# The low part of one weight unit moved from VectorE to GpSimd, in the last head of an mLSTM mixer

## The reference, cut to what matters

```python
ha = rmsnorm(ha, lw['norm_mlstm_h'].reshape(H_A, DV_A)).reshape(B, T, D_MODEL)
y_a = jax.nn.sigmoid(oa) * ha
...
merged = jax.nn.sigmoid(ga) * y_a + jax.nn.sigmoid(gb) * y_b
return merged @ lw['w_out'], (ckv, kr, C, n, m)
```

## Time and profile before

| | us |
|---|---|
| median of 3 runs | 1330.66 |
| lowest and highest run | 1329.96, 1330.77 |
| time of the profiled execution | 1328.88 |
| its span | 1327.2 |

### The profile page before, as it was taken

The page is one execution under the profiler, slowest core; times in us unless marked ns, Lnnn a source line. Parts: engine busy times, 40 slices in busy tenths (PEclk is TensorE's granted clock), DMA queues, the critical chain, the costliest instruction groups (busy, mean ns, idle before and its releaser), DMA issues.

```text
span 1327.2 us, 30517 instructions
## 1 busy us (share of the span) xinstructions
PE 1300.7 (98%) x11657; PEld 1232.1 (93%) x11657; DVE 959.8 (72%) x1847; ACT 602.2 (45%) x1144; POOL 145.9 (11%) x275
## 2 busy tenths in 40 slices
PE   9999999999999999999999999999999999999997
PEld 9999999999999988888888888889899999999996
DVE  5999889985487564554554665574889989988556
ACT  6455555653365344444344223324654555565323
POOL 0000000000003105555552000000000000000000
PEclk9999999999999999999999999999999999999999
DMA  4232223333156637778777323415152222333322
GB/s 177 83 126 98 96 96 124 109 95 95 60 192 223 214 94 219 243 216 245 212 227 261 113 78 115 153 48 193 59 186 96 96 96 97 107 111 111 96 88 101
DMA packets 86235, 180.85 MB, mean 136 GB/s; under 512 B 12682, under 2 KB 47499, under 8 KB 84043
## 3 DMA queue, kind: packets, MB, share of 16 engines
q1 hardware_dynamic: 77466, 160.55, 36.1%
q0 software_dynamic: 8192, 16.79, 4.6%
q10 hardware_dynamic: 432, 1.57, 0.4%
HBM read 162.29 MB, written 16.57 MB: 135 GB/s over the span
## 4 chain that ended last, share of the span: by engine, by line
PE 77%; DVE 9%; issue 6%; DMA 3%; POOLq 2%; ACT 2%; POOL 1%; SPq 0%; DVEq 0%; ACTq 0%
PE acc L1093 20%; PE acc L1178 14%; PE acc L1015 11%; PE bank_a L1093 6%; PE acc L852 6%; PE acc L1039 4%; POOLq L475 2%; PE acc L924 2%; DVE w_lo L2330 1%; PE bank_a L1248 1%; DMA w_raw<-in_w_gu 1%; PE bank_a L1278 1%; DVE x L2384 1%; PE acc L1070 1%; PE acc L1296 1%
## 5 line engine op out<-in xcount | busy, mean ns | idle before, releaser
L1093 PE MATMUL acc<-x_forms,pair_w 128*128 128x272 f32 x1728 | 273.1, 288 | 0.0
L1093 PEld LDWEIGHTS acc<-x_forms,pair_w 128*128 128x128 f32 x1728 | 244.2, 188 | 0.0
L1178 PE MATMUL acc<-x_hi,w_hi 128*128 128x272 f32 x656 | 198.3, 302 | 0.2 <-DVE gt L2805 0.2
L1178 PE MATMUL acc<-x_hi,w_lo 128*128 128x272 f32 x656 | 190.9, 291 | 0.0
L1178 PE MATMUL acc<-x_lo,w_hi 128*128 128x272 f32 x656 | 190.4, 290 | 0.0
L2330 DVE TENSOR_TENSOR w_lo<-w_raw,w_hi 128x1024 fp32r<-128x1024 f32 (+1 forms) x92 | 108.2, 1176 | 93.2 <-ACT w_hi L1624 92.8
L493 POOL DMA_DIRECT2D pg<-in_lat x256 | 138.6, 542 | 191.2 <-issue 132.7
L1624 ACT ACTIVATE w_hi<-w_raw 128x1024 fp32r<-128x1024 f32 (+1 forms) x92 | 93.0, 1018 | 91.3 <-PE acc L1178 38.9
L1178 PEld LDWEIGHTS acc<-x_hi,w_hi 128*128 128x128 f32 x656 | 123.6, 188 | 8.2 <-issue 6.4
L1178 PEld LDWEIGHTS acc<-x_lo,w_hi 128*128 128x128 f32 x656 | 123.7, 189 | 3.9 <-issue 3.0
L1178 PEld LDWEIGHTS acc<-x_hi,w_lo 128*128 128x128 f32 x656 | 123.5, 188 | 2.5 <-issue 2.2
(11 more groups left out here) (454 smaller groups left out, 2847.4 us busy)
## 6 DMA issues: line engine op xcount, KB each, us to landing
w_pair<-in_w_gu SPq DMA_DIRECT2D x68, 512.0 KB, 4.2
pg<-in_key_t SPq DMA_DIRECT2D x256, 96.0 KB, 2.6
w_raw<-in_w_in SPq DMA_DIRECT2D x44, 512.0 KB, 4.6
pg<-in_lat POOLq DMA_DIRECT2D x256, 64.0 KB, 2.8
w_raw<-in_w_dn SPq DMA_DIRECT2D x32, 448.0 KB, 3.3
w_raw<-in_w_gu SPq DMA_DIRECT2D x20, 512.0 KB, 3.9
block_raw<-in_w_dn SPq DMA_DIRECT2D x32, 256.0 KB, 3.6
g_mid<-gt SPq DMA_DIRECT2D x17, 272.0 KB, 3.0
```

The source lines that it names most:

```text
L1093: ins = nc.tensor.matmul(bank, w[:, k * P:(k + 1) * P], v[:, k, :], start=start and k == 0 and term == 0, stop=k == KD // 2 - 1 and term == 2,
L1178: ins = nc.tensor.matmul(acc[0][:, a, 0:HT], w[:, i % 2, k * P:(k + 1) * P], v[:, k, a * HT:(a + 1) * HT], start=k == 0 and term == 0, sto ...
```

## The change

VectorE no longer makes the low part of unit 1 of the output projection. GpSimd makes it, in its loop over the heads, in the last head, ahead of that head's factors. It waits for the high part of the unit (`w_hi`) and for the slot (`w_used`), and counts `w_split` as VectorE did.

```diff
@@ -3265,7 +3265,6 @@
                     split_merged(2)
                     split_merged(3)
                     dense(1)
-                    next_unit("out", 0, 0)
                 else:
                     dense(fill)
                 if h == 0:
@@ -3374,6 +3373,12 @@
             ins.then_inc(vtok_ones, 1)
             pool.wait_ge(pchain, 2)
             for h in range(HA):
+                if h == HA - 1:
+                    U = STAGE["out"][0] + 1
+                    pool.wait_ge(w_hi, U + 1)
+                    pool.wait_ge(w_used, U - 1)
+                    nc.gpsimd.tensor_tensor(wlo[:, U % 2, 0:KD * P], raw[:, U % 2, 0:KD * P],
+                                            f32(whi[:, U % 2, 0:KD * P]), ALU.subtract).then_inc(w_split, 1)
                 pool.wait_ge(ss_ready, (NT + 1) * (h + 1))
                 nc.gpsimd.tensor_scalar(ssr[:, 1, 0:NT + 1], ssr[:, 0, 0:NT + 1], 1.0 / DV, EPS, ALU.mult, ALU.add)\
                     .then_inc(pchain, 1)
```

## The result

The changed kernel took 1331.33 us in the median of 18 runs, the kernel before 1329.36 us in 18 runs: a ratio of 1.0013, with a 95% interval of 1.0007 to 1.0019. The profiled execution took 1330.19 us with a span of 1328.5 us, against 1328.88 and 1327.2 before.

A forecast was written before the change was run, and what follows sets the result against it. TensorE's matmuls were busy for 98% of the span, with VectorE the bound for about one microsecond in the last head. 1328.88 + 1.19 = 1330.07 us profiled, plus 1.78 to the median, rounded to 1331.9 us; range 1329.1 to 1333.0.

The forecast's parts named there:

- The sign and the mechanism: Last head: slower, as GpSimd's subtraction takes the SBUF port between the two L3229 and holds the second until 887.09 us.
- The subtraction's length: GpSimd's low part of 1024 columns in the last head: 2.24 us, range 0.95 to 2.66.
- The shift: L3216 (outputs(6)) in the last head starts 1.19 us later, and the delay stays to the end.
- the seam: Last head, where TensorE's L1503 waits for VectorE, about one microsecond; measured from first L3229 to head_out's first matmul.
- The gain at most: TensorE's wait ahead of L1503 that the removal from VectorE could save: at most 0.95 us.
- The covers: Last head: factors queued behind the subtraction come at worst at 889.1 us, before VectorE's L3174 needs them at 890.9.
- Rival A: Last head: the engines don't hold each other up, so TensorE gains 0.95 us: 1329.7 us; chance 0.26.
- Rival B: Last head: GpSimd always gives way, subtraction and factors come late, L3174 waits: about +0.6 us, 1331.3; chance 0.12.
- Rival C: Last head: every GpSimd instruction holds the port to its end, the power L3381 too: +2.43 us, 1333.1; chance 0.05.
- Rival D: Last head: slower by more than 0.2% through a subtraction longer than 3.71 us; at 4.5 us, 1334.1; chance 0.05.
- The predicted time: Whole kernel: median 1331.9 us, from a profiled 1330.07 plus the 1.78 us the median stood above it; chance 0.52.

The follow-up runs named there:

- 8 columns: Changed kernel with GpSimd subtracting only 8 of the 1024 columns, the rest of that low part left out; ratio 0.999 to the kernel before.
- memset: Changed kernel with GpSimd writing zeros to the whole 128x1024 tile in place of the subtraction; first L3229 to head_out's first matmul took 6.13 us.
- copy: Changed kernel with GpSimd copying the raw unit into the tile in place of the subtraction; first L3229 to head_out's first matmul took 6.99 us.

## Why the prediction was right, step by step

- **The sign and the mechanism** came out as forecast: GpSimd got in at the border of the two L3229, and the second one ran behind it. The forecast stood on a row that showed only the opposite direction (L3378's 0.60 us); that the hold works both ways was an assumption there, and the runs with 8 columns, a memset and a copy have now shown it.
- **The subtraction's length** was put at 2.24 us between bounds of 0.95 and 2.66; it took 2.35 us where it ran without being held, and 887.16 - 884.85 = 2.31 us from the border. The Trainium skill's figure (GPSIMD Engine Reference, 3.1 Elementwise — side-by-side cycle accounting), 2.25 us by estimate, agrees to 0.1 us. As worked out from the rows, the 2.24 is in part luck: it is the middle of two bounds built from streams of 0.83 ns a column, one behind the other, and the runs do not bear that picture out. The copy, which reads one stream and writes one, took 0.99 us from the border, 0.04 us more than the memset, which only writes; the subtraction, with a second read, took 1.32 us more than the copy, not 0.85. Where that time goes is not shown.
- **The shift** was 1.19 us by the sum and 1.04 by the seam. The subtraction ended where it was forecast: 887.09, against 887.16 in an execution that was 0.09 us later at this place. The term that was a little too large is the stretch from there to L3216: 1.75 us in the sum, and 888.77 - 887.16 = 1.61 in the trace. Of these 0.14 us, 0.08 lie in the sum itself, which counts the second L3229 from its start at 884.77 although the hold begins at the first one's end, 884.85. The other 0.06 is VectorE going on before the end that the trace gives the subtraction.
- **The gain at most** of 0.95 us, taken from TensorE's wait, was 1.11 in the run that isolates it. Without the wait, L1503 starts before the end that the trace gives the matmuls ahead of it: at 888.47 with 8 columns, and they end at 888.22 + 0.41 = 888.63. These 0.16 us are what the forecast left out when it let L1503 start at their end.
- **The covers held.** The factors ended at 887.88 + 1.24 = 889.12 us (889.1 forecast as the worst case), and L3174 started at 890.84 without waiting for them. The cover has an end: with the subtraction behind L2818 they cost 2.02 us of VectorE's time.
- **Rival A** (no collision) would be right for a writer: the memset gave its -1.14 us. **Rival B** did not happen by itself. **Rival C**, the rule that the prediction cites from the Trainium skill (SBUF — State Buffer, Who interferes with whom), that the hold lasts a whole instruction, is half right. The hold on L3229 lasted for nearly all of the subtraction, up to 0.06 to 0.14 us before its end. But the power L3386 (887.88 to 889.12) held nobody, since L2818 beside it took 0.73 us. **Rival D** needed 3.71 us of subtraction.
- **The predicted time**, 1331.9 us, stands against 1331.33. Part of that closeness is luck: the baseline's median was 1329.36 in 18 runs, not 1330.66, and the difference of the medians, 1.97 us, is larger than the seam that explains it.

## What to carry to other kernels

Before a float32 elementwise instruction goes to GpSimd for relief, look at what VectorE does beside it. Here instructions with SBUF operands only (L3229, L2817, L2818) waited for nearly as long as GpSimd's subtraction, copy or piece ran, while L3216, which reads one operand from PSUM, and the memset, which only writes, did not meet; other kinds of instruction were not run. An instruction that takes 1.2 us on VectorE and 2.3 on GpSimd must find 2.3 us beside which VectorE does not meet it. Where TensorE waits for VectorE at one place, first try to move the work one step back in VectorE's own order, and to put the wait for it where it is used; here that was worth 0.9 us at the seam, and the other engine cost 1.0.

## What the runs showed of the hardware that was not expected

- A held instruction shows as a long one, not as idle time: VectorE's busy time rose from 959.8 us to 961.1 although an instruction of 1.22 us was taken from it: the held L3229 alone is longer by 2.17 (the row on the engines stands at the end). The same shows on GpSimd, where a factor instruction on 128x5 takes 0.20, 0.34, 0.55 or 0.60 us, depending on its neighbours.
- L2817, with a single tensor operand in SBUF and a constant, is held as well: 0.97 us between the four pieces instead of 0.44. The rows ahead of the prediction showed only a VectorE instruction with two SBUF operands in such a meeting. The Trainium skill (SBUF — State Buffer, Who interferes with whom) counts such instructions in when they run in a fast two-port mode. L2817 takes 0.44 us for the 544 columns for which L2818 takes 0.72, which would fit such a mode, but whether L2817 runs in that mode is not shown by these runs.
- Let go means between instructions: four pieces of 256 columns took turns with three VectorE instructions, one each, although the pieces were queued back to back.

The busy times on the page of the changed kernel:

```profile
PE 1301.3 (98%) x11657; PEld 1232.6 (93%) x11657; DVE 961.1 (72%) x1846; ACT 603.3 (45%) x1144; POOL 150.3 (11%) x276
```

DVE has one instruction less than before and is busy for longer. POOL has one more and is busy for 4.4 us longer: 2.54 are the subtraction's, and most of the rest stands in the 256 instructions of L493, far ahead of the seam, which took 140.5 us instead of 138.6 (138.3 with 8 columns).
